# Experts 30 and 31 of a mixture of experts: one joint scatter, sums in two PSUM banks each, output by column halves

## The reference

```
logits = h @ w_router + b_router;  top_val, top_idx = top_k(logits, 4);  gates = softmax(top_val)
for expert e, rows xe = the tokens that chose e:
    gu  = xe @ w_gate_up[e] + b_gate_up[e]            # 1024 -> 2 x 1024
    g   = min(gu[:, :1024], 7);  u = clip(gu[:, 1024:], -7, 7)
    y   = ((u + 1) * g * sigmoid(1.702 g)) @ w_down[e] + b_down[e]
out[token] += gate[token, e] * y
return x + gate2 * out                                # gate2: one factor per column
```

## Time and profile before

| | us |
|---|---|
| time, median of 3 runs | 2262.51 (2259.31 to 2262.86) |
| the profiled execution | 2261.65 |
| its span | 2259.9 |
| TensorE busy | 2192.0 (97%) |
| VectorE, ScalarE busy | 964.9 (43%), 679.6 (30%) |

### The profile page before, as it was taken

One profiled execution on the slowest core, in us unless ns is written; L12 is line 12 of the kernel. 1 busy time (PEld: TensorE's weight loads), 2 busy tenths in 40 slices (PEclk: granted clock), 3 DMA queues, 4 the chain that ended last, 5 costly groups with the idle time before them and its releaser, 6 DMA issues. The chain is left out here.

```text
span 2259.9 us, 29771 instructions
## 1 busy us (share of the span) xinstructions
PE 2192.0 (97%) x12161; PEld 1322.1 (59%) x12162; DVE 964.9 (43%) x1387; ACT 679.6 (30%) x1095; POOL 92.4 (4%) x139
## 2 busy tenths in 40 slices
PE   8999999999999999999999999999999999999998
PEld 7887776788788867768887753333333333333332
DVE  4563684666575438547549752221111111112111
ACT  4432332544343323244335641111111111111111
POOL 5000020000000001100002000000000000000000
PEclk9999999999999999999999999999999999999999
DMA  8763421776387442148744579999999999999998
GB/s 296 245 233 99 148 77 39 242 261 226 109 284 262 164 143 75 40 131 282 267 177 139 197 286 424 428 428 429 427 429 429 427 428 429 429 427 428 429 429 351
DMA packets 192725, 632.36 MB, mean 280 GB/s; under 512 B 31281, under 2 KB 127553, under 8 KB 166257
## 3 DMA queue, kind: packets, MB, share of 16 engines
q1 hardware_dynamic: 192624, 630.93, 72.4%
HBM read 629.82 MB, written 1.07 MB: 279 GB/s over the span
## 5 line engine op out<-in xcount | busy, mean ns | idle before, releaser
L410 PE MATMUL banks<-ffn_room 128*128 128x512 f32 x1920 | 453.7, 392 | 0.0
L410 PEld LDWEIGHTS banks<-ffn_room 128*128 128x128 f32 x1920 | 357.5, 188 | 72.8
L527 DVE TENSOR_TENSOR ffn_room<-memory,ffn_room 128x2048 fp32r<-128x2048 f32 x124 | 281.0, 2292 | 99.5 <-ACT ffn_room L487 99.4
L3064 DVE TENSOR_SCALAR attend_words<-banks 128x512 f32<-128x512 f32 x32 | 22.1, 691 | 564.0 <-PE banks L2800 564.0
L487 ACT CAST ffn_room<-memory 128x2048 fp32r<-128x2048 f32 x124 | 232.2, 1903 | 70.7 <-PE banks L428 62.8
L428 PE MATMUL banks<-ffn_room 128*128 128x512 f32 x1056 | 248.1, 390 | 0.3
L2800 PE MATMUL banks<-memory 128*64 128x512 f32 x1088 | 243.9, 596 | 0.0
L428 PEld LDWEIGHTS banks<-ffn_room 128*128 128x128 f32 x1056 | 197.6, 188 | 42.7 <-DVE ffn_room L566 2.1
L2800 PEld LDWEIGHTS banks<-memory 128*64 128x64 f32 x1088 | 75.4, 136 | 151.9 <-issue 150.1
L2800 PE MATMUL banks<-attend_later,memory 128*64 128x512 f32 x672 | 152.0, 594 | 0.1
L493 ACT ACTIVATE memory<-banks 128x256 f32<-128x256 f32 x88 | 33.8, 385 | 341.7 <-PE banks L410 318.9
(11 more groups left out here) (440 smaller groups left out, 2463.9 us busy)
## 6 DMA issues: line engine op xcount, KB each, us to landing
memory<-in_ffn_w SPq DMA_DIRECT2D x132, 1024.0 KB, 7.4
memory<-in_w_gate_up SPq DMA_DIRECT2D x62, 2048.0 KB, 22.3
attend_later<-in_w_gate_up SPq DMA_DIRECT2D x39, 2048.0 KB, 23.8
memory<-in_w_down SPq DMA_DIRECT2D x25, 2048.0 KB, 24.2
attend_later<-in_w_down SPq DMA_DIRECT2D x19, 2048.0 KB, 23.2
attend_words<-in_w_gate_up SPq DMA_DIRECT2D x17, 2048.0 KB, 22.3
memory<-in_w_in SPq DMA_DIRECT2D x32, 1024.0 KB, 6.2
memory<-in_w_ada SPq DMA_DIRECT2D x32, 768.0 KB, 5.1
```

The lines of the kernel that those rows point to most:

```text
L410: m = nc.tensor.matmul(psum[:, GU + tt, :], x_parts[:, xp, k, tt * P:tt * P + P], rows, start=(n == 0), stop=(n == 3 * KD - 1))
L527: tt_op(b, chip.ring[:, chip.slot(base + i), :], a.bitcast(F32), ALU.subtract).then_inc(chip.used, 1)
L3064: ts(room.gate, psum[:, GATE_BANK, :], 7.0, None, ALU.min).then_inc(s["g_ready"], 1)
```

## The change

Up to expert 29's rows nothing moves except one step of VectorE. For experts 30 and 31:

- `down_both` takes the place of `down`. All products of expert 30 go to partitions 0 to 63 (`halves[0]`) and all of expert 31 to partitions 64 to 127 (`halves[1]`). The left and right output columns now lie in two banks in place of on two halves of the partitions: banks Y and UP for expert 30, GATE and Y for expert 31. For a tile the order is block 0 left, block 1 left, block 0 right, block 1 right; for the last tile block 0 left and right, then (when its second half has landed) block 1 left and right. The product that completes the left sums counts up `left_done`.
- `weigh_half` multiplies by `gate2` over 64 partitions and 512 columns, four times, in place of `take_down` over 128 partitions, twice. The results form `ye_both[0]` and `ye_both[1]`: 128 rows, of which the upper 64 are expert 31's.
- `scatter_both` takes the place of two scatters: a contraction over all 128 rows for both experts at once, left columns of both token tiles first, then the right ones.
- `select_back_both` fills `back` for both experts ahead of expert 31's hidden values, so the second `select_back`, `turn_back` and `take_back` go.
- `swap_gate2` exchanges the column halves of `gate2` on partitions 64 to 127 by three copies (one copy in `tables` before), behind expert 0's hidden values.
- The output is stored as left and right columns of all 256 tokens in place of as token halves.

```diff
@@ sync
-            sp.wait_ge(s["first_rows"], 2)
-            store(chip, sp, routed, out, 0, chip.stored)
-            sp.wait_ge(s["last_rows"], 2)
-            store(chip, sp, routed, out, 1, chip.stored)
+            for h, done in enumerate((s["left_out"], s["right_out"])):
+                sp.wait_ge(done, 2)
+                cols = slice(h * HALF, h * HALF + HALF)
+                sp.dma_start(out[0:1, :, cols].rearrange("b (t p) d -> p (b t) d", p=P), routed.acc[:, :, cols])\
+                  .then_inc(chip.stored, 16)
@@ tensor
+            def down_both(e, j0, tiles):
+
+                room_half, banks = (halves[0], (Y_BANK, UP_BANK)) if e == LAST else (halves[1], (GATE_BANK, Y_BANK))
+                if tiles[0] == 0:
+                    pe.wait_ge(s["act"], e)
+                    if e == LAST:
+                        pe.wait_ge(s["ye"], LAST - 1)
+                for i in tiles:
+                    pe.wait_ge(*landed(e, j0 + i))
+                    tile = slot(e, j0 + i)
+                    late = e == NE and i == D4 - 1
+                    order = [(0, 0), (0, 1), (1, 0), (1, 1)] if late else [(0, 0), (1, 0), (0, 1), (1, 1)]
+                    for c, h in order:
+                        k = 2 * i + c
+                        if late and (c, h) == (1, 0):
+                            pe.wait_ge(s["last_half"], 16)
+                        if i == 0 and (c, h) == (0, 1):
+                            pe.wait_ge(*((s["gu_read"], NE) if e == LAST else (s["ye"], LAST)))
+                        m = mm(psum[room_half, banks[h], :], act_rows(e - 1)[:, k, :], block_of(tile, c, h),
+                               start=(k == 0), stop=(k == KD - 1))
+                        if late and (c, h) == (1, 0):
+                            m.then_inc(s["left_done"], 1)
+                    m.then_inc(chip.used, 1)
...
+            def scatter_both():
+
+                for h in range(2):
+                    pe.wait_ge(s["ye"], LAST + 2 + h)
+                    for tt in range(NT):
+                        m = mm(psum[:, ACC + 2 * tt + h, :], room.scatterT[:, tt, :], room.ye_both[h],
+                               start=False, stop=True, skip_group_check=True)
+                    m.then_inc(s["scat" if h else "scat_first"], 1)
...
-            down(LAST, G8, (0, 1))
+            down_both(LAST, G8, (0, 1))
             turn_hidden(LAST)
-            down(LAST, G8, (2, 3))
-            down(NE, 0, (0,), GATE_BANK)
-            scatter(LAST)
-            turn_back(NE)
-            down(NE, 0, (1, 2, 3), GATE_BANK)
-            scatter(NE)
+            down_both(LAST, G8, (2, 3))
+            down_both(NE, 0, range(D4))
+            scatter_both()
@@ scalar
-            take_back(NE)
             act.wait_ge(s["scat_first"], 1)
-            copy(routed.acc[:, 0, 0:512], psum[:, 0, :]).then_inc(s["first_rows"], 1)
-            act.wait_ge(s["scat"], NE)
-            copy(routed.acc[:, 1, 0:512], psum[:, 2, :]).then_inc(s["last_rows"], 1)
+            copy(routed.acc[:, 0, 0:512], psum[:, 0, :]).then_inc(s["left_out"], 1)
+            act.wait_ge(s["scat"], LAST)
+            copy(routed.acc[:, 0, 512:1024], psum[:, 1, :]).then_inc(s["right_out"], 1)
@@ vector
+            def weigh_half(i, bank, h, at):
+
+                p = halves[i]
+                tt_op(room.ye_both[h][p, :], psum[p, bank, :], routed.gate2[p, at * HALF:at * HALF + HALF], ALU.mult)\
+                    .then_inc(s["ye"], 1)
+
+            def swap_gate2():
+
+                dve.wait_ge(s["hidden"], 1)
+                p, g = halves[1], routed.gate2
+                chain(nc.vector.tensor_copy(room.up[p, :], g[p, 0:HALF]))
+                chain(nc.vector.tensor_copy(g[p, 0:HALF], g[p, HALF:2 * HALF]))
+                chain(nc.vector.tensor_copy(g[p, HALF:2 * HALF], room.up[p, :]))
...
-                nc.vector.tensor_copy(routed.gate2[halves[1], 0:HALF], routed.gate2[halves[1], HALF:2 * HALF])
...
             activate(0)
+            swap_gate2()
...
-            select_back(LAST)
+            select_back_both()
             activate(LAST)
-            take_down(LAST, taken(LAST, LOADS))
-            select_back(NE)
-            take_down(NE, taken(NE, D4), GATE_BANK)
+            dve.wait_ge(s["hidden"], NE)
+            dve.wait_ge(chip.used, taken(LAST, LOADS))
+            dve.wait_ge(s["scat"], LAST - 1)
+            weigh_half(0, Y_BANK, 0, 0)
+            weigh_half(0, UP_BANK, 1, 1)
+            dve.wait_ge(s["left_done"], 1)
+            weigh_half(1, GATE_BANK, 0, 1)
+            dve.wait_ge(chip.used, taken(NE, D4))
+            weigh_half(1, Y_BANK, 1, 0)
             dve.wait_ge(s["scat_first"], 1)
-            nc.vector.tensor_copy(routed.acc[:, 0, 512:1024], psum[:, 1, :]).then_inc(s["first_rows"], 1)
-            dve.wait_ge(s["scat"], NE)
-            nc.vector.tensor_copy(routed.acc[:, 1, 512:1024], psum[:, 3, :]).then_inc(s["last_rows"], 1)
+            nc.vector.tensor_copy(routed.acc[:, 1, 0:512], psum[:, 2, :]).then_inc(s["left_out"], 1)
+            dve.wait_ge(s["scat"], LAST)
+            nc.vector.tensor_copy(routed.acc[:, 1, 512:1024], psum[:, 3, :]).then_inc(s["right_out"], 1)
```

More of the change, by code:

```diff
@@ L2528 @@
 EXPERTS = ("gates tables_turned gatesT down_rows xe_low xe_first sel_first chain picked gu_read g_ready sig gated hidden sel back back_turned back_out gathered rows_out rows_turned xe "
-           "turned act ye scat last_half down_bias tables scat_first first_rows last_rows")
+           "turned act ye scat last_half down_bias tables left_done scat_first left_out right_out")
 def reach(eng, sem, value):
@@ L2563, in __init__ @@
         self.ye = self.xe = wide.take(HALF)
+        self.ye_both = (self.ye, self.up)
 class LateRoom:
@@ L2824, in down @@
                         k = 2 * i + c
-                        if in_halves(e, i) and c == 1:
-                            pe.wait_ge(s["last_half"], 16)
                         for h in range(2):
@@ L2830, in down @@
                     m.then_inc(chip.used, 1)
-            def in_halves(e, i):
-                return isinstance(e, int) and e == NE and i == D4 - 1
+            def down_both(e, j0, tiles):
[20 more added lines that the diff above has]
+                    m.then_inc(chip.used, 1)
             def turn_back(e):
@@ L2903, in scatter @@
                                start=False, stop=True, skip_group_check=True)
-                    if tt == 0 and isinstance(e, int) and e == NE:
-                        m.then_inc(s["scat_first"], 1)
                 m.then_inc(s["scat"], 1)
+            def scatter_both():
[5 more added lines that the diff above has]
+                    m.then_inc(s["scat" if h else "scat_first"], 1)
             def add_bias():
@@ L3035, in take_first_gathered @@
                            routed.shiftT[:, k:k + 1], ALU.mult, ALU.add).then_inc(s["xe_low"], 1)
+            chain = Chain(dve, s["chain"])
             def weights_of_tokens():
-                chain = Chain(dve, s["chain"])
                 st = chip.stats
@@ L3055, in select_back, with select_back_both @@
                 m.then_inc(s["back"], 1)
+            def select_back_both():
+                dve.wait_ge(s["back_turned"], LAST - 1)
+                for tt in range(NT):
+                    for i, e in enumerate((LAST - 1, LAST)):
+                        m = ts(room.back[:, tt, CAP * i:CAP * i + CAP], routed.iota[:, 0:CAP], routed.place[:, tt, e:e + 1],
+                               routed.gates[:, tt, e:e + 1], ALU.is_equal, ALU.mult)
+                m.then_inc(s["back"], 1)
+            def weigh_half(i, bank, h, at):
[8 more added lines that the diff above has]
+                chain(nc.vector.tensor_copy(g[p, HALF:2 * HALF], room.up[p, :]))
             def pick(e):
@@ L3271 @@
 FFN_STEP = 256
-WIDE_SET, SLIM_SET = 100, 32
+WIDE_SET, SLIM_SET = 100, 33
 START = "chain ident x c turned"
```

## The result

| | before | after |
|---|---|---|
| median of 10 runs each | 2262.46 (2257.37 to 2266.24) | 2268.63 (2265.32 to 2273.47) |
| profiled execution, its span | 2261.65, 2259.9 | 2273.47, 2271.8 |
| first down product of expert 30 to the span's end | 26.5 | 35.3 |

The forecast was +9.4 us and 2271.9 us. The profiled execution of the changed kernel is the slowest of its ten, and its span is 11.9 us above that of before. So the third line of the table is needed: it counts from the start of the stretch that the change rearranges (2233.40 before, 2236.47 after). The stretch is 8.8 us longer.

The account below looks back on a forecast made before the run. Weight transfers set the expert phase's pace; TensorE's chain sets the end. Products +9.0 us, left first -0.8, scatter +1.7, stores -0.4 gave about +9.4: 2271.05 profiled, plus 0.86 for the median, 2271.9 us; range 2269.4 to 2274.6.

Parts of the forecast that it names:

- The price of a down product: Down products of experts 30 and 31: on one half, two steps of 0.43 us each, 27.5 us where before 13.8.
- Reading (b): Down products: a pair is two records of one product, the half doesn't matter; no change, 2262.3 us; 6%.
- Loads exposed: Down products and scatter: weight loads on one half can't hide, 9.0 us and 1.1 us more; 2282 us; 3%.
- rival 2: Slower still: 64 down records pay 0.14 us more each for weight loads, the scatter 1.1 us; 2282 us; 3%.
- The covered wait: Expert 31's first tile: its second-column product, at 2249.7, finds expert 30's first multiplication done by 2248.9, so no cost.
- step 6: Edits taken at nothing: gate swap, joint selection and expert 30's multiplications, all expected to be hidden behind other work.
- The scatter: Joint scatter at the end: 8 records in 8 steps, 3.73 us in place of 2.01, costing 1.7.
- left first: Last tile's left columns complete two steps before the end, so the left scatter starts earlier; gives back 0.8 us.
- Copies and stores: After the scatter: last copy takes 0.69 us, then 3.5 us less 0.4 to the span's end.
- the 0.4 of the queue: Two final stores: issued 1.7 us apart in place of 0.86, the second no longer queues, saving 0.4 us.
- pieces of 2 KB: Final stores in 2 KB pieces in place of 4 KB: may cost 0 to 1.2 us, taken as 0.

Follow-up runs that it names:

- e1: Changed kernel with left products back on partitions 0 to 63, right on 64 to 127, for both experts; ratio to before 1.0003, stretch 27.0 us.
- e4: Kernel before with all down products of experts 30 and 31 on partitions 0 to 63; ratio to before 1.0044, stretch 37.9 us.
- e2: Changed kernel with expert 31's right sums in the shared bank, without the wait for expert 30's left multiplication; ratio to before 1.0036, stretch 34.4 us.
- e5: Changed kernel with the joint scatter waiting for both of expert 31's multiplications; stretch 36.2 us, one run of 2269.00 us on another chip.
- e6_turn_early: Kernel before with only expert 31's selection and turn moved earlier, turned gates in their own buffer; stretch 26.2 us, one run of 2264.24 us.
- e3: As e2, with expert 30's fourth down tile and expert 31's first issued alternately, product by product; ratio to before 1.0022, stretch 31.8 us.

## Why the prediction was right, point by point

The times from the first down product of expert 30 on, in us:

| | forecast | measured |
|---|---|---|
| first two tiles | 6.93 | 7.0 |
| last down product ends | 28.5 | 27.7 |
| left scatter starts | 28.4 | 27.7 |
| right scatter ends | 32.1 | 31.4 |
| last copy ends | 32.8 | 32.1 |
| span ends | 35.9 | 35.3 |

- *The price of a down product* was right, to 0.01 us in a step. The nearest row was that of two lines of another layer, with products of 64 x 64; it held for products of 512 columns. Those rows were weaker evidence than the prediction says: by its code L1001 alternates the half of the array's rows together with the half of its columns (`psum[r, ...], lhsT[r, ...]`), so they can't tell which of the two makes the pair. e1, which changes the output's half alone, does. Reading (b) is refuted by the timeline and by e1 and e4.
- *Loads exposed* (rival 2) didn't come: the loads lie behind the running record, 0.14 us each, and the step is still 0.43. The rule of the Trainium skill ("TensorE: Matmul & The Clock Gate", "The mechanism"), that loads overlap only with products in another group of rows, disagrees with these rows.
- *The covered wait* of step 6 was the largest error, and its two parts partly cancel. I had expert 31's right product at 2249.7, behind a multiplication done at 2248.9. I took the products to run in the order of the list. Expert 31's first two products ran beside the end of expert 30's, which saved four steps, 1.7 us, so TensorE came to the wait before the multiplication was done and stood there for 0.77. With the end and the start of a run the stop costs 0.94: the next record starts at 2251.96, where 2251.02 was its turn. The 1.72 less the 0.94 are the 0.8 by which the end of the products came earlier than forecast. e2 confirms the cost of the wait. That the sum came so near is in this part luck: the overtaking was not foreseen.
- *The scatter* took 3.65 to 3.70 (forecast 3.73), and *left first* gave 0.8 (forecast 0.8; e5).
- *Copies and stores*: 3.2 us from the last copy to the end, forecast 3.1. Each of the two stores now lands 2.8 us after its issue; before, the first took 2.7 and the second, queued behind it, 3.1. So the 0.4 of the queue is gone, as forecast, and pieces of 2 KB cost 0.1 us at most.
- *swap_gate2* lies, with its three copies, ahead of a selection that TensorE's turn (L2861) needs; the last copy ends 5.4 us ahead of that turn, as these two rows show.

```profile
1373.58 0.43 DVE L3102 COPY kept<-attend_words 64x512 f32<-64x512 f32 x1
...
1379.37 0.44 PE L2861 MATMUL banks<-memory 128*128 128x128 f32 x2
```

The forecast of the time, 2271.9, is 3.3 above the measured median; 0.6 of that is the stretch. The rest is within what the runs of one kernel differ by: the medians moved by 6.2 where the stretch grew by 8.8. The scatter ahead of the stretch, told of in the last section, is large enough for it; that it is the cause is not shown.

## What to carry to other kernels

The down products here have 64 output partitions, and which half of the array's columns they use goes by those partitions. Giving one expert all of one half turns every pair of products into a sequence: 16 records take 7.05 us, where 8 by turns take 1.94. Before merging two small products into one wider (here the scatters, where the last one takes 3.70 us in place of 1.99), count the steps and not the instructions: two products on two halves took the steps of one already. And at the end of a phase that is bound by transfers, what counts is the work that is left after the last byte: 10.45 us of products here, and 2.2 before.

## What the runs showed of the hardware

Two things were not expected.

TensorE starts products of another half ahead of those that stand before them in its list: with three records of expert 30 still to start, the first of expert 31 began (2249.25 against 2249.67, 2250.10 and 2250.53 in the changed kernel; e2, e3 and e5 have three records still to start as well). So "nothing is reordered" holds for the list as it is written and not for the starts on the two halves. How far ahead TensorE can start, and what sets that, is not shown.

The 3.1 us that the profiled execution of the changed kernel lost before the stretch lie at one place, at the entry to the expert phase. A group of 16 records of L1954 starts at 1324.69 before and at 1324.43 in the changed kernel, 0.26 us earlier; the first 32 records of gate and up products (L2800, now L2802) start at 1349.56 and 1352.34, 2.8 later. The stretch from 1335 to 1350 us, columns as in rows 2, in the kernel before, in the changed one, and in e2_own_bank:

```profile
1335.00:1350.00 15.00, 14.70 (x65) 9.99 (x66) 5.66 (x30) 4.66 (x13) 0.00 (x0) 0.77 0.48 184
```

```profile
1335.00:1350.00 15.00, 14.70 (x52) 9.56 (x52) 3.76 (x22) 2.96 (x9) 0.00 (x0) 0.54 0.45 176
```

```profile
1335.00:1350.00 15.00, 14.51 (x78) 8.33 (x79) 5.82 (x30) 4.56 (x13) 0.00 (x0) 1.00 0.47 182
```

It isn't the change: e2_own_bank has the changed kernel's code there and a clock of 1.00, e6_turn_early that of before and 0.56. The longer TensorE runs at 1.2 there, the later the down stage of experts 30 and 31 begins: e2 and e5, at 1.00, have their first down product at 2230.1 and 2231.1 us, e1 at 0.89 at 2232.1, before at 2233.4, e3 and e4 at 0.66 at 2235.3 and 2235.0, and e6 at 0.56 at 2236.4 and the changed kernel at 0.54 at 2236.5. That is 6.4 us from one execution to another, beside the 8.8 that the change costs. Why the clock is at 1.2 GHz there for longer in one execution than in another is open. Whoever compares two profiled executions of this program by their spans compares this first.
